# A decode step with turned attention weights: pieces at other places, their PSUM banks emptied by ScalarE

## What is computed

```python
kc = compress(rows[:, :, 0], cmp_w1[0], cmp_w2[0], cmp_pe[0])   # keys and values of 32-token windows
vc = compress(rows[:, :, 1], cmp_w1[1], cmp_w2[1], cmp_pe[1])
o_cmp, p = cmp_attention(q, kc, vc, qpos)                        # 255 compressed keys
sel = select_blocks(p, qpos, kb.shape[2])                        # the 16 best blocks of 64 tokens
o_slc = selected_attention(q, kb, vb, sel, qpos)                 # "chosen"
o_win = window_attention(q, win_cat[:, :, 0], win_cat[:, :, 1], qpos, kpos)   # "newest" 512 tokens
o_nsa = nsa_combine(o_cmp, o_slc, o_win, ngates, ngate)
```

## Time and profile before

| | |
|---|---|
| median of three runs | 2114.49 us |
| the profiled execution, its own time | 2107.58 us |
| its span | 2105.8 us |
| mean granted TensorE clock | 0.983 |
| busy: TensorE, VectorE, ScalarE, GpSimd | 1971.9, 882.5, 735.3, 565.1 us |
| decode loop, TensorE busy of 1147 to 1840 us | 588.71 of 693.00 us |
| ScalarE busy there | 425.94 us |
| one sample (first TURNED at 1309.36 us, seventh at 1837.60) | 88.0 us |

### The profile page before, as it was taken

One profiled execution on the slowest core, in us unless ns is written; L12 is line 12 of the kernel. 1 busy time (PEld: TensorE's weight loads), 2 busy tenths in 40 slices (PEclk: granted clock), 3 DMA queues, 4 the chain that ended last, 5 costly groups with the idle time before them and its releaser, 6 DMA issues. The chain is left out here.

```text
span 2105.8 us, 25188 instructions
## 1 busy us (share of the span) xinstructions
PE 1971.9 (94%) x9303; PEld 1356.8 (64%) x9303; DVE 882.5 (42%) x1781; ACT 735.3 (35%) x1345; POOL 565.1 (27%) x585
## 2 busy tenths in 40 slices
PE   8999999999999999999996898888888888899997
PEld 7888888888888887777774454444444444444442
DVE  0354545454531014444445355454554545511127
ACT  0231133213310003223323665666566665510013
POOL 0000000000002003343345476656466565030000
PEclk9999999999999999999998999999999999999999
DMA  5222222222222321111114555547374563563224
GB/s 199 89 80 91 91 71 80 91 91 71 80 82 102 100 95 48 61 41 41 41 41 140 170 160 171 168 156 218 107 211 143 176 214 111 196 241 142 80 80 161
DMA packets 76486, 248.95 MB, mean 118 GB/s; under 512 B 11764, under 2 KB 35520, under 8 KB 62176
## 3 DMA queue, kind: packets, MB, share of 16 engines
q1 hardware_dynamic: 46312, 148.04, 20.4%
q0 software_dynamic: 28800, 95.45, 15.0%
q10 hardware_dynamic: 1280, 4.23, 0.5%
HBM read 225.17 MB, written 22.49 MB: 118 GB/s over the span
## 5 line engine op out<-in xcount | busy, mean ns | idle before, releaser
L292 PE MATMUL pj<-xT,strips 128*128 128x260 f32 x2368 | 533.2, 384 | 6.3 <-DMA xT<-d_xT 6.3
L292 PEld LDWEIGHTS pj<-xT,strips 128*128 128x128 f32 x2368 | 446.4, 191 | 72.3 <-issue 6.2
L1869 ACT ACTIVATE big<-dtb 64x512 f32<-64x512 f32 x512 | 302.9, 592 | 164.0 <-PE dtb L1601 152.3
L792 PE MATMUL pj<-xT,strips 128*128 128x260 f32 x1216 | 291.0, 387 | 0.0
L1624 PE MATMUL dpH<-big,w 128*128 128x512 f32 x512 | 274.3, 621 | 0.9 <-DVE hs L1992 0.9
L792 PEld LDWEIGHTS pj<-xT,strips 128*128 128x128 f32 x1216 | 222.0, 190 | 59.1 <-issue 29.6
L1975 DVE TENSOR_TENSOR big<-big 128x512 f32<-128x512 f32 x128 | 88.1, 689 | 217.9 <-ACT big L1869 217.9
L1018 POOL MEMSET kbd<- 128x128 f32 x1 | 0.2, 204 | 635.9 <-POOLq L126 635.9
L1044 POOL TENSOR_SCALAR old<-old,rd 128x128 f32<-128x128 f32 (+3 forms) x116 | 122.0, 1066 | 166.8 <-DVE rd L1153 166.8
L1601 PEld LDWEIGHTS dtb<-const,xT 128*128 128x128 f32 x512 | 66.3, 150 | 127.8 <-issue 86.9
L1567 POOL DMA_INDIRECT KV<-d_cache,gi x104 | 102.4, 985 | 169.4 <-DVE gi L2111 140.1
(11 more groups left out here) (312 smaller groups left out, 2345.4 us busy)
## 6 DMA issues: line engine op xcount, KB each, us to landing
strips<-d_w_in SPq DMA_DIRECT2D x60, 1024.0 KB, 5.1
xT<-d_w_out SPq DMA_DIRECT2D x16, 1024.0 KB, 7.7
d_win_sample<-Wt SPq DMA_DIRECT2D x8, 1024.0 KB, 7.3
Xr<-d_w_out SPq DMA_DIRECT2D x8, 1024.0 KB, 8.6
Wt<-d_win SPq DMA_DIRECT2D x8, 896.0 KB
oT<-d_cache SPq DMA_DIRECT2D x84, 80.0 KB
xT<-d_xT SPq DMA_DIRECT2D x8, 520.0 KB, 9.8
Sold<-d_state SPq DMA_DIRECT2D x8, 512.0 KB, 5.2
```

Source lines behind the costliest of these rows:

```text
L292: mm = nc.tensor.matmul(pj[b][:, a, 0:TH], w[b][:, k, :], xT[:, k, a * TH:(a + 1) * TH], start=(k == 0), stop=(k == KT - 1))
L792: mm = nc.tensor.matmul(bank(s)[:, n, 0:TH], w[s % 2][:, k, :], xT[:, k, n * TH:(n + 1) * TH], start=(k == 0), stop=(k == KT - 1))
L1869: ins = A(dst[:, :, :, hd], tb[bank][hd * DH:(hd + 1) * DH].rearrange("p (j h n) -> p j h n", j=2, h=2), ACT.Copy)
```

## The change

Three edits. The table AT has new places. GpSimd's first four gathers go out ahead of its memsets. The functions that empty the banks of turned weights stand in ScalarE's program and not in VectorE's, with activations in place of copies; the waits and semaphores are the same, and each is run at its piece's place.

```diff
         AT = {
-            "queries": 19, ("second", 0): 27, ("second", 1): 29, "scores": 31, "weights": 35, "sums": 37,
-            "first": 38, "turned": 40, "values": 41, "slots": 42, "bases": 43, "rows": 48,
-            ("second", 2): 53, "fetch0": 54, ("second", 3): 55, "keys0": 58, "mix": 59, "fetch1": 61, "acc": 62,
-            "keys1": 64, "fetch2": 73, "keys2": 76, "fetch3": 80, "keys3": 82,
-            "SCORES": 87, "SCALE": 92, "TURNED": 94, "VALUES": 97, "NEWEST0": 99, "NEWEST1": 100,
-            "WSCORES": 105, "WSCALE": 108, "WTURNED": 111, "WVALUES": 113, "SUM": 114, "DONE": 118,
+            "queries": 19, ("second", 0): 26, ("second", 1): 29, "scores": 31, "weights": 35, "sums": 37,
+            "first": 38, "values": 41, "slots": 42, "bases": 43, "turned": 46, "rows": 48,
+            ("second", 2): 53, "fetch0": 54, ("second", 3): 56, "keys0": 57, "mix": 59, "fetch1": 61, "acc": 62,
+            "keys1": 63, "fetch2": 73, "keys2": 75, "fetch3": 78, "keys3": 81,
+            "SCORES": 87, "SCALE": 92, "NEWEST0": 93, "NEWEST1": 99, "TURNED": 100, "VALUES": 103,
+            "WSCORES": 106, "WSCALE": 108, "WTURNED": 112, "WVALUES": 114, "SUM": 117, "DONE": 124,
         }
...
-            for n in range(2):
-                nc.gpsimd.memset(qbd[n][:], 0.0).then_inc(init, 1)
-            nc.gpsimd.memset(pn[:], 0.0).then_inc(init, 1)
-            nc.gpsimd.memset(sc[:], FORCED).then_inc(init, 1)
...
-            for q in range(4):
+            rows(0, 0, 0)
+            for n in range(2):
+                nc.gpsimd.memset(qbd[n][:], 0.0).then_inc(init, 1)
+            nc.gpsimd.memset(pn[:], 0.0).then_inc(init, 1)
+            nc.gpsimd.memset(sc[:], FORCED).then_inc(init, 1)
+            for q in range(1, 4):
                 rows(0, q, 0)
...
+            def chosen_turned(b):
+                bank, k = place["TURNED", b]
+                act.wait_ge(tr[bank], k + 1)
+                A(packed(PTg[:, 0:NT - 1]), picked(bank, P, 0, NT - 1), ACT.Copy)
+                A(packed(PTg[0:SL + 1, NT - 1:NT]), picked(bank, SL + 1, NT - 1, 1), ACT.Copy).then_inc(pts_e, 1)
+                act.wait_ge(pts_e, b + 1)
+                act.sem_inc(ev[bank], 1)
...
-            def chosen_turned(b):
-                bank, k = place["TURNED", b]
-                v.wait_ge(tr[bank], k + 1)
-                V.tensor_copy(packed(PTg[:, 0:NT - 1]), picked(bank, P, 0, NT - 1))
-                V.tensor_copy(packed(PTg[0:SL + 1, NT - 1:NT]), picked(bank, SL + 1, NT - 1, 1)).then_inc(pts_e, 1)
-                v.wait_ge(pts_e, b + 1)
-                v.sem_inc(ev[bank], 1)
```

More of the change, by code:

```diff
@@ L1904, in scores, with packed, picked, turned @@
                   accum_out=col[:, 2:3]).then_inc(e_c, 1)
+            def packed(t):
+                return t.rearrange("p t (h r) -> p t h r", h=2)
+            def picked(bank, n, t, m):
+                return tb[bank][0:n, t * 64:(t + m) * 64].rearrange("p (t h r) -> p t h r", h=2, r=32)[:, :, :, 0:2 * G]
+            def turned(b):
+                bank, k = place["turned", b]
+                act.wait_ge(tr[bank], k + 1)
+                A(packed(PTc[:, 0:1]), picked(bank, P, 0, 1), ACT.Copy)
+                A(packed(PTc[0:NCMP - P, 1:2]), picked(bank, NCMP - P, 1, 1), ACT.Copy).then_inc(ptc_e, 1)
+                act.wait_ge(ptc_e, b + 1)
+                act.sem_inc(ev[bank], 1)
+            def chosen_turned(b):
+                bank, k = place["TURNED", b]
+                act.wait_ge(tr[bank], k + 1)
+                A(packed(PTg[:, 0:NT - 1]), picked(bank, P, 0, NT - 1), ACT.Copy)
+                A(packed(PTg[0:SL + 1, NT - 1:NT]), picked(bank, SL + 1, NT - 1, 1), ACT.Copy).then_inc(pts_e, 1)
+                act.wait_ge(pts_e, b + 1)
+                act.sem_inc(ev[bank], 1)
+            def newest_turned(b):
+                bank, k = place["WTURNED", b]
+                act.wait_ge(tr[bank], k + 1)
+                A(packed(PTw[:]), picked(bank, P, 0, WIN // P), ACT.Copy).then_inc(ptw_e, 1)
+                act.wait_ge(ptw_e, b + 1)
+                act.sem_inc(ev[bank], 1)
             def chosen_scores(b):
@@ L1953, in _ @@
                 "scores": scores, "SCORES": chosen_scores, "WSCORES": newest_scores,
+                "turned": turned, "TURNED": chosen_turned, "WTURNED": newest_turned,
                 **{FETCH[q]: fetch(q) for q in range(4)}, **key_pieces(act)})
@@ L2018, in second @@
                     V.tensor_copy(vc[:, par, :], pK[:, 0:KVH * DH]).then_inc(k2_e, 1)
[L2020 to L2025, removed]
             def queries(b):
@@ L2052, in weights @@
                                 ALU.add).then_inc(imp_r, 1)
-            def turned(b):
-                bank, k = place["turned", b]
-                v.wait_ge(tr[bank], k + 1)
-                V.tensor_copy(packed(PTc[:, 0:1]), picked(bank, P, 0, 1))
-                V.tensor_copy(packed(PTc[0:NCMP - P, 1:2]), picked(bank, NCMP - P, 1, 1)).then_inc(ptc_e, 1)
-                v.wait_ge(ptc_e, b + 1)
-                v.sem_inc(ev[bank], 1)
             def sums(b):
@@ L2248, in _ @@
                 "product": product, "turn": turn, "output": output, "end": add,
-                "second": second, "queries": queries, "scores": scores, "weights": weights, "turned": turned,
+                "second": second, "queries": queries, "scores": scores, "weights": weights,
                 "sums": sums, "first": first, "values": values, "acc": weigh, "slots": slots, "bases": bases,
-                "rows": rows, "SCORES": chosen_scores, "WSCORES": newest_scores, "TURNED": chosen_turned,
-                "WTURNED": newest_turned, "SCALE": chosen_scaled,
+                "rows": rows, "SCORES": chosen_scores, "WSCORES": newest_scores, "SCALE": chosen_scaled,
                 "WSCALE": newest_scaled, "SUM": add_up, "DONE": done, **{FETCH[q]: fetch(q) for q in range(4)}})
```

## The result

The changed kernel takes 2057.61 us (median of four runs, 2057.15 to 2060.21), the kernel before, beside it, 2113.76 us (four runs, 2111.83 to 2121.23). The ratio is 0.973, with a 95% interval of 0.9705 to 0.9755. The forecast was 2058.0.

What follows compares the result with a forecast made beforehand. TensorE's waits and half-clock periods bound the loop: 107.6 us, of which 51.0 come back. 2107.6 less 56.6 and GpSimd's 0.8 gives 2050; the profile lies 6.9 under the median, so 2057, plus 1 for ScalarE: 2058 us; range 2032 to 2094.

Steps and rivals of the forecast that it cites:

- The old waits: TensorE's waits in the decode loop, in six main groups; new places were to remove them, TURNED's 22.9 us the largest.
- Items 1 to 4: New loop waits: after SCORES 14.2 us, WSCORES 6.0, other set of sums 15.9, second `second` 4.0 and L1704's sums 3.0.
- The slow periods: Ten half-clock TensorE periods in the loop, costing 17.1 us; three were to stay, costing 5.1 us.
- the seven slow periods with them: Seven half-clock periods following TURNED waits were to go when TURNED moved behind SCALE, 11.9 us.
- Rival A: Short TensorE waits keep the clock falling: ten slow periods stay, 2070 us, or two in each of seven samples, 2077; 18%.
- ScalarE for VectorE: ScalarE's three bank emptyings per sample cost nothing on the path, or 8 us if its lag is not made up.
- rival B: ScalarE's queue becomes the loop's bound, costing TensorE 4 to 5 us more per sample: 2090 us; 13%.
- the gathers leave 0.77 us earlier: At the stage's start, GpSimd's first gathers go ahead of its memsets and TensorE waits for them: 0.8 us gained.
- Item 5: Removing the last TURNED wait, 2.8 us, buys nothing: VectorE then stands in the first output tile until x lands.
- second: One more place, 0.86 us, between the halves of `second`; half of each 1.1 us wait was taken as gained.
- C: Late landing of the first chosen blocks makes the kernel slower than before, 2128 us; 5%.
- D: New waits in the loop replace the old nearly one for one, 2104 to 2114 us; 7%.

Runs made afterwards that it cites:

- Experiment 1: The kernel before with only the new table of places, VectorE still emptying the banks and memsets first: 2067.91 us, ratio 0.9775.
- experiment 2: The kernel before with only ScalarE in place of VectorE for the three banks, old places and old GpSimd order: 2124.96 us, ratio 1.0045.
- experiment 4: The changed kernel with GpSimd's memsets ahead of its first gathers again: 2056.36 us, ratio 0.9719.
- Experiment 8: The changed kernel with the last sample's fourth `second` back at 55 and the previous sample's VALUES at 104: 2050.84 us; separately, TURNED back at 94: 2076.81 us.

## Why the prediction was right, and where it was not

The time was forecast at 2058.0 and is 2057.61. For the loop this is no accident: gained were to be 56.6 us plus 2.8 that belong to the end, 59.4, and the loop gained 61.9. That the time came out within 0.4 us is luck. The end grew by 12.0 us where 2.8 were put, and the start by 2.5 where 0.8 were to be gained, 12.5 us the wrong way. Against them stands the step from the profile to the median: the forecast added 6.9 us, as if every kernel's median lay so far above its profile, and 1 more for ScalarE. But, going by the granted clocks, the 6.9 were slow periods of before that its profile happened not to have; the median of after lies 2.6 us under its profile. This error, 10.5 us, and the 2.5 of the loop cancelled the others. Step by step:

**The old waits.** All six groups went. Experiment 1 shows that the places did it, and experiment 2 that ScalarE alone does not. The reason given, two places until the bank's next turn in place of one, fits `turned`, keys0 and DONE, 35.6 us, but it can't be the reason for WTURNED, which had two places before as well and cost 8.9 us. Experiment 1 leaves 1.1 of these with VectorE still emptying, one place later, and experiment 2 leaves none at the old place. And `turned` on VectorE waits 11.2 us in experiment 1 though it has two places. So the room that a bank needs depends on what stands ahead in the queue of the engine that empties it.

**What is late next.** Items 1 to 4 put back 43.1 us; 40.9 came. The kinds were right as well: turns behind ScalarE, up to 1.3 us, the join in fifteen waits of up to 1.2, keys of the second `second` 5.8, the sums of L1704 2.1.

**The slow periods.** Three were to stay and two did. But the step "the seven slow periods with them", which tied them to TURNED's long wait alone, is wrong as a mechanism. Moving TURNED alone took the wait away and the clock did not rise (16 periods in the profile; a median clock of 0.9765 against 0.978). Putting it back among the new places brought eight. A long wait thus has them behind it, also in a loop with few others, but a loop full of waits of 0.7 to 2.3 us has as many without it. The number came out right because the change removes the other waits in the same samples too. Rival A, that the new short waits keep the clock falling, did not come about: some eight waits of up to 1.3 us per sample, two periods. The Trainium skill (TensorE: Matmul & The Clock Gate, A second HAM failure mode: psum-queue depth-cycling) says that frequent short idle moments make the clock swing. The kernel with TURNED alone (waits of up to 2.3 us, 16 periods) agrees with it, the changed kernel (waits of up to 1.3 us, two) does not. Which pattern of waits makes the clock fall stays open.

**ScalarE for VectorE.** Put at nothing on the path, with up to 8 us against it. Its copies are as short as estimated and it is not the bound (rival B): it is busy 425 of 615 us. The step missed something in its favour: at place 46 VectorE would empty `turned` late and cost 11.2 us, which the sum had not weighed since it took the two edits together. Experiment 1 puts that at 7.5 us of loop net, and beside experiment 4 at 11.6 us in all. One sign of the forecast missed: ScalarE is busy 1.3 us more over the loop, not about 10.

**GpSimd.** Put at 0.8 us, measured at nothing, 0.1 us in the gathers' start. The failed step is "the gathers leave 0.77 us earlier": the gather begins 0.6 us behind the stage's first matmul even with nothing ahead of it, as the timeline of experiment 4 shows.

**The end.** Item 5 put back 2.8 us, since a wait would be exchanged for the one for x. What came is 9.1 us of wait and 3.1 of lower clock, and the end 12.0 us longer. The step that failed is the one on *second*: it counted one more place between its halves, 0.86 us, and did not follow that place into the last sample, where it crosses from the loop into the output tiles and behind a join that waits for x. Experiment 8 takes it away and gets 7.5 us back of 12.2 for wait and clock: a wait of 2.8 us for keys, which hangs on x too, comes forth behind it, and one slow period (1.7) stays, which leaves 0.2 us open.

**Rivals C and D.** In the changed loop TensorE waited for a landing once, at its start, so C's late blocks never came; D, new waits one for one, is excluded by 40.9 against 90.5.

## What to carry to other kernels

Count the steps from each buffer's use to its next one, and beside them what stands ahead in the queue of the engine that empties it: one step of 0.86 us was too little here, two were enough with a free engine and not with a busy one (11.2 us for `turned` on VectorE). Mend all of them at once: the table as a whole carried most of the gain, while TURNED moved alone gave nothing that could be told from no change. When a table of places is edited, walk it through the last round as well and look whether a piece crosses an operation that waits for a load in the same in-order queue; here one place cost 7.5 us. Look at what else hangs on that load before calling it free. When a wait is removed, count the slow-clock periods beside the waits, since the clock can take back much of it, and compare the granted clock over all executions before reading one profile: before's ranged from 0.975 to 0.983, which is 17 us.

## What the runs showed of the hardware

The granted clock's slow periods don't go by the longest wait alone: a loop whose longest wait had fallen from 3.3 to 2.3 us had 16, at a median clock no higher than before's (0.9765 against 0.978), and one had 26 with 6 us less of waiting in all. What a wait costs therefore depends on its company: the same wait of TURNED was worth 2.9 us of loop in one kernel and 26.0 in another (by medians, 1.4 and 19.2 us).

Going by the mean granted clock, the same program on the same chip has different numbers of slow periods from one execution to the next: before's 21 executions lie at a mean granted clock of 0.975, of 0.977 to 0.979, or of 0.981 to 0.983, and at 2105.90 to 2123.11 us.

ScalarE's small copies out of PSUM took 190 to 263 ns for 16 to 112 columns, and a gather's issue at the start of a stage stands 0.6 to 0.7 us behind its first matmul whether four memsets precede it or not.

The chips differ: the same program before took 2114 to 2120 us in three measurements and 2266 and 2304 in two others, on other chips, there with idle moments of up to 15 us on ScalarE that the profile puts down to no instruction; why was not found.
